# Page scores of the sample group: the queries held still on four column quarters, the turned keys of four pages moving, and the scores turned back

## Chip, core and metric

The kernel runs on one core of a Trainium2 chip. The metric is the time of one execution on the device in microseconds (us). Engines are named as in the profile: PE is TensorE (PEld its weight loads), DVE is VectorE, ACT is ScalarE, POOL is GpSimd, SP issues DMAs.

## The reference

One step of a decoder trunk of two layers. A prompt of 1024 new tokens and 8 sample sequences with one new token each (and 2048 past positions in 16 pages of 128) share all weights. Layer 0 mixes tokens by stick-breaking attention, layer 1 by forgetting attention; both have 16 heads of 64 with 4 key/value heads, and each layer ends in a convolutional feed-forward part.

```
h = rms_norm(x, norm_mix[i]);  q, k, v = split_qkv(h @ w_qkv[i])
k_all = concat(gather_pages(cache_k[i], page_table), k)       # sample group: 16 pages + 1 new row
z = einsum('bqngd,bsnd->bngqs', q, k_all) * Dh**-0.5          # the scores that the change is about
stick:  log_keep = log_sigmoid(-z);  w = exp(log_sigmoid(z) + sum of log_keep over later positions)
fox:    w = softmax(z + cum[pos] - cum[s])
x = x + einsum('bngqs,bsnd->bqngd', w, v_all) @ w_o[i]
x = x + conv_ffn(rms_norm(x, norm_ffn[i]))
```

The change touches z of the sample group alone: for each of 8 samples one query of 16 heads against 16 pages of 128 keys.

## The kernel before

Activations are kept transposed in SBUF, 1024 prompt columns and 8 sample columns. `attention(l)` is one phase per layer in which five engines run programs written out by hand; semaphores alone order them across engines, and each engine works strictly in its own order.

The prompt's attention goes in 128 steps: 16 heads of 8 query blocks of 128 rows. Within a head the blocks come in the order `ORDER = (0, 7, 1, 6, 2, 5, 3, 4)`, so a step at an odd place has a block index of 4 to 7, and one at an even place of 0 to 3. A step N of block i has (i+1) x 128 keys. On PE a turn of the loop for step N is: `turn(N)` (transposes of the weights in `rows`, one PSUM bank for every four key blocks, so one group for i below 4 and two from 4 on), then page transposes of the step, then `scores(N+3)`, then `values(N-1)`, then page scores. ACT and DVE empty the turned banks alternately into `wt` (`copy_turned`). In layer 0, ACT computes two sigmoids of the scores (`mid`), DVE a running product over them (`read_scores`, a scan), POOL a product. In layer 1, DVE adds the decay and takes the maximum (`read_scores`, a reduction), ACT the exponential, DVE the reciprocal, POOL the scaling. DVE reads the scores of step N+2 ahead of its copies of step N; one step before a new head's first scores are needed it also rounds that head's queries (`prepare`), and at each new key head the keys.

The samples' work is strewn over the same steps. A unit is two pages of a sample's keys; there are 64 units in a layer, at steps 2 to 59 (`k_step`). For a unit, SP loads two pages (`kpage`, six buffers), PE turns them (`turn_keys`, four 128x128 transposes into one bank), ACT copies the bank to `kt`, of which there are two, and one step later PE scores them (`score_keys`): the turned keys are stationary, 128 columns of them, and the 8 queries of a half of the heads in `qd` move. The result has keys on partitions and heads on columns, as all that follows needs it. After the 8 units of a sample DVE copies its scores from PSUM to `score` (`copy_scores`). Then come sums over later pages or the softmax, and from step 72 the value pages (`sum_values`).

All turned things share three PSUM banks, `t_ps`, in the order of the list `groups`. A group takes the bank of the third group before it, so `bank_free(g)` lets PE wait until ACT or DVE has copied that one:

```
def bank_free(g):
    if g >= TB:
        wait_copied(pe, g - TB)
```

Of the kernel before, what the change touches and what calls it, by code (L numbers as in the profile page):

```python
# [20 lines left out]
P = 128  # L21
# [8 lines left out]
def trunk_program(nc, x_prompt, x_sample, cache_k, cache_v, cache_logf, state_conv, page_table,  # L30
# [26 lines left out]
    with ctx:  # L57
# [1007 lines left out]
        UNITS = NB * NPAGE // 2  # L1065
        SEQ_UNITS = NPAGE // 2
        ROWS = 4
# [16 lines left out]
        def attention(l):  # L1084
# [20 lines left out]
            score = tile("score", [P, NB, NP1, NH])  # L1105
            qd = tile("qd", [P, HALVES, NB, HH])
            pages = tile("pages", [1, NB * NPAGE], I32)
# [7 lines left out]
            else:  # L1115
# [3 lines left out]
            kpage = [at(f"kpage{j}_{l}", [P, 2, KVD], XH + 4 * TILE + j * 2 * KVD * 4) for j in range(K_SLOTS)]  # L1119
            kt = [at(f"kt{j}_{l}", [P, 4 * P], XH + 4 * TILE + (K_SLOTS * KVD + j * 2 * P) * 8) for j in range(2)]  # L1120
            assert K_SLOTS * 2 * KVD * 4 + 2 * 4 * P * 4 <= 4 * TILE
            vpage = [at(f"vpage{j}_{l}", [P, 2, KVD], R1 + j * 2 * KVD * 4) for j in range(V_SLOTS)]
# [14 lines left out]
                [sem(f"dc_values{j}_{l}") for j in range(V_SLOTS)]  # L1137
            s_qd, s_ks, s_ev = sem(f"dc_queries_{l}"), sem(f"dc_scores_{l}"), sem(f"dc_scores_copied_{l}")
            s_ca, s_cd, s_cp = sem(f"dc_act_{l}"), sem(f"dc_dve_{l}"), sem(f"dc_pe_{l}")
# [9 lines left out]
            v_step = [V_FIRST + u * V_OVER // UNITS for u in range(UNITS)]  # L1149
            SCORED = k_step[-1] + 1  # L1150
            CUM = SCORED + 2 if fox else PER_TURN + 2
# [3 lines left out]
            def units_at(table, N):  # L1155
                return [u for u in range(UNITS) if table[u] == N]

            groups, of_step, of_unit = [], {}, {}
            for N in range(STEPS):
                for j0 in range(0, ORDER[N % ST] + 1, 4):  # L1160
                    of_step.setdefault(N, []).append(len(groups))
                    groups.append((j0, "act" if sum(1 for g in groups if g[0] is not None) % 2 == 0 else "dve"))
                for u in units_at(k_step, N):
                    of_unit[u] = len(groups)
                    groups.append((None, "act"))

            def copies(g):
# [30 lines left out]
            with phase() as block:  # L1198
# [27 lines left out]
                def _(pe):  # L1226
# [44 lines left out]
                    def turn_keys(u):  # L1271
                        g = of_unit[u]
                        bank_free(g)
                        pe.wait_ge(s_kp[u % K_SLOTS], 32 * (u // K_SLOTS + 1))
                        for j in range(2):
                            for hf in range(HALVES):
                                last = nc.tensor.transpose(t_ps[g % TB][:, (2 * j + hf) * P:(2 * j + hf + 1) * P],
                                                           kpage[u % K_SLOTS][:, j, hf * P:(hf + 1) * P], ident[:, :])
                        last.then_inc(s_t, 1)

                    def score_keys(u):
                        b, n = u // SEQ_UNITS, 2 * (u % SEQ_UNITS)
                        if u == 0:
                            pe.wait_ge(s_qd, 2)
                            if fox:
                                pe.wait_ge(s_tail, 2)
                        if n == 0 and b >= 1:
                            pe.wait_ge(s_ev, b)
                        wait_copied(pe, of_unit[u])
                        for j in range(2):  # L1290
                            for hf in range(HALVES):
                                c = b % 2 * NPAGE * NH + (n + j) * NH + hf * HH
                                last = nc.tensor.matmul(dec[:, c:c + HH], kt[u % 2][:, (2 * j + hf) * P:(2 * j + hf + 1) * P],
                                                        qd[:, hf, b, :], start=True, stop=True)
                        last.then_inc(s_ks, 1)

                    def score_new():
                        pe.wait_ge(s_qd, 2)
                        for b in range(NB):
                            for hf in range(HALVES):  # L1300
                                c = (b * HALVES + hf) * HH
                                last = nc.tensor.matmul(dec[0:1, c:c + HH], kvT[:, hf, SEQ + b:SEQ + b + 1], qd[:, hf, b, :],
                                                        start=True, stop=True)
                        last.then_inc(s_tail, 1)

                    def sum_keys(c):
                        if c == 0:
                            pe.wait_ge(s_ev, NB)
                            pe.wait_ge(s_cd, SUMS)
                        else:  # L1310
                            pe.wait_ge(s_cd, SUMS + c)
# [26 lines left out]
                    for N in range(STEPS + 1):  # L1338
# [6 lines left out]
                        if N >= 1:  # L1345
                            values(N - 1)
                            for u in units_at(k_step, N - 1):
                                score_keys(u)
                        for u in units_at(v_step, N):
# [18 lines left out]
                def _(dve):  # L1368
# [67 lines left out]

                    def copy_scores(b):
                        dve.wait_ge(s_ks, SEQ_UNITS * (b + 1))
                        src = dec[:, b % 2 * NPAGE * NH:(b % 2 + 1) * NPAGE * NH].rearrange("p (n h) -> p n h", h=NH)
                        nc.vector.tensor_copy(score[:, b, 0:NPAGE, :], src).then_inc(s_ev, 1)  # L1440

# [82 lines left out]
                    for side in range(2):  # L1524
                        for par in range(2):
                            last = nc.vector.tensor_copy(
                                qd[half(side)].rearrange("p f b (s j r) -> p f s j r b", s=2, j=2)[:, :, side, :, par, :],
                                sample_columns(qT, side, par))
# [11 lines left out]
                    for N in range(STEPS + 1):  # L1540
                        if fox and N + 1 < STEPS:
                            invert(N + 1)
                        if N + 2 < STEPS:
                            read_scores(N + 2)
                        if N < STEPS:
                            copy_turned(N)
                        if heads_prepared_at(N) is not None:
                            prepare(heads_prepared_at(N))
                        if N >= 1 and (N - 1) % ST >= ST - 2:
                            store_o(N - 1)  # L1550
                        for u in units_at(k_step, N - 1):
                            if u % SEQ_UNITS == SEQ_UNITS - 1:
                                copy_scores(u // SEQ_UNITS)
                        if fox and N == PER_TURN - ST:
# [11 lines left out]
                def _(act):  # L1566
# [46 lines left out]
                    def copy_keys(u):  # L1613
                        g = of_unit[u]
                        if u >= 2:
                            act.wait_ge(s_ks, u - 1)
                        act.wait_ge(s_t, g + 1)
                        nc.scalar.activation(kt[u % 2][:, :], t_ps[g % TB][:, :], ACT.Copy).then_inc(s_ta, 1)

                    def soft_plus():  # L1620
                        act.wait_ge(s_ev, NB)
                        act.wait_ge(s_q, 2 * HG)
# [26 lines left out]
                    ahead = 2 if fox else 3  # L1649
                    for N in range(STEPS):  # L1650
                        copy_turned(N)
                        for u in units_at(k_step, N):
# [77 lines left out]
```

## Time and profile before

| | |
|---|---|
| three runs | 3201.16, 3202.53, 3210.64 us, median 3202.53 |
| the profiled execution | 3201.7 us, its span 3199.7 us |
| busy in the span | PE 3002.5 us (94%), DVE 1401.9 (44%), ACT 901.0 (28%), POOL 888.6 (28%) |

The page gives busy time by engine, the granted clock of PE in tenths of full speed, and the costliest groups of instructions. PE is busy nearly everywhere, so what the change makes PE do counts at once, and what it lets PE wait for counts too; the other engines have room, and only the moment at which they get to a thing matters.

### The profile page before, as it was taken

Reading aid. Unit: us, or ns where it says so; the run is one execution under the profiler, and the core shown is the slowest. Engines: PE = TensorE matmul, PEld = TensorE weight load, DVE = VectorE, ACT = ScalarE, POOL = GpSimd, SP = SyncE. Lnnn points to the kernel's source line nnn. Section 1 sums busy time; section 2 is a strip of 40 time slices with the busy share of each in tenths; the row PEclk is TensorE's granted clock in tenths of the full one; section 3 lists DMA queues with packets and bytes.
Section 4 is the critical chain, followed back from the end, with each engine's and each line's share of the span. In section 5 each row is a group of like instructions: output and inputs, shape, how many; then the busy total and the mean of one; then the engine's idle time right before and its main releaser. Section 6 shows DMA issues by size and latency. Waiting matters only on the chain. (4 is left out here: it accounts for less than half of the span.)

```text
span 3199.7 us, 50554 instructions
## 1 busy us (share of the span) xinstructions
PE 3002.5 (94%) x19894; PEld 2870.9 (90%) x19894; DVE 1401.9 (44%) x1823; ACT 901.0 (28%) x1229; POOL 888.6 (28%) x415
## 2 busy tenths in 40 slices
PE   6989997998999999999999899899899999999994
PEld 5978886888999999999989789788899999999994
DVE  5144445554434334334361444655443433343435
ACT  3035554443211111111230354433321121111111
POOL 2112222332122322222311244445312222222220
PEclk8989897999999999999999899999999999999997
DMA  2112211221111111111101233133111111111111
GB/s 99 55 54 65 65 41 47 83 84 53 40 40 53 47 51 47 39 39 53 54 31 48 82 102 94 56 110 106 57 40 40 40 53 53 53 39 39 40 39 53
DMA packets 177557, 182.75 MB, mean 57 GB/s; under 512 B 31927, under 2 KB 167569, under 8 KB 177334
## 3 DMA queue, kind: packets, MB, share of 16 engines
q1 hardware_dynamic: 175086, 172.14, 17.5%
q10 hardware_dynamic: 2304, 8.39, 0.8%
q8 instruction: 104, 1.70, 0.2%
q14 instruction: 63, 0.52, 0.1%
HBM read 171.67 MB, written 8.99 MB: 56 GB/s over the span
## 5 line engine op out<-in xcount | busy, mean ns | idle before, releaser
L334 PE MATMUL psum<-x_hi,w_hi 128*128 128x344 f32 x2688 | 578.1, 324 | 4.2 <-issue 2.7
L334 PE MATMUL psum<-x_lo,w_hi 128*128 128x344 f32 x2688 | 571.9, 321 | 0.0
L334 PE MATMUL psum<-x_hi,w_lo 128*128 128x344 f32 x2688 | 569.0, 320 | 0.0
L334 PEld LDWEIGHTS psum<-x_hi,w_hi 128*128 128x128 f32 x2688 | 451.7, 189 | 7.5 <-issue 4.7
L334 PEld LDWEIGHTS psum<-x_lo,w_hi 128*128 128x128 f32 x2688 | 456.2, 190 | 0.0
L334 PEld LDWEIGHTS psum<-x_hi,w_lo 128*128 128x128 f32 x2688 | 449.6, 188 | 0.0
L867 DVE TENSOR_TENSOR xT<-psum,xT 128x1032 f32<-128x1032 f32 x176 | 217.0, 1233 | 287.2 <-PE psum L334 287.2
L713 POOL TENSOR_TENSOR w_lo<-raw,w_hi 128x2048 fp32r<-128x2048 f32 x44 | 203.3, 4621 | 419.9 <-ACT w_hi L709 419.9
L1267 PE MATMUL psum<-wt,tokv 128*64 128x128 f32 x2304 | 319.2, 286 | 0.0
L1671 POOL TENSOR_SCALAR rows<-rows,stat 128x128 f32<-128x128 f32 (+7 forms) x128 | 220.5, 1726 | 309.8 <-DVE stat L1420 309.7
L854 POOL TENSOR_TENSOR act_lo<-gate,act_hi 128x1032 fp32r<-128x1032 f32 x44 | 106.3, 2415 | 717.5 <-ACT act_hi L825 717.5
L1267 PEld LDWEIGHTS psum<-wt,tokv 128*64 128x64 f32 x2304 | 255.9, 141 | 31.9 <-issue 12.0
L1678 POOL TENSOR_TENSOR rows<-rows,keep 128x128 f32<-128x128 f32 (+7 forms) x128 | 154.3, 1214 | 434.5 <-DVE keep L1403 434.5
L334 PE MATMUL psum<-act_hi,down_hi 128*128 128x344 f32 x1056 | 225.6, 322 | 12.8 <-issue 12.8
L334 PE MATMUL psum<-act_hi,down_lo 128*128 128x344 f32 x1056 | 225.4, 322 | 0.0
L334 PE MATMUL psum<-act_lo,down_hi 128*128 128x344 f32 x1056 | 223.8, 320 | 0.0
L1403 DVE TENSOR_TENSOR_SCAN keep<-psum,zero 128x128 f32<-128x128 f32 (+7 forms) x128 | 173.3, 1355 | 114.2 <-ACT psum L1601 112.9
L875 DVE TENSOR_TENSOR a_pad<-psum,rstd 128x1032 f32<-128x1032 f32 x44 | 54.2, 1233 | 384.2 <-PE psum L334 384.2
L709 ACT ACTIVATE w_hi<-raw 128x2048 fp32r<-128x2048 f32 x44 | 84.4, 1918 | 416.0 <-DMA raw<-in_ffn_w_b_dram 209.5
L1239 PE MATMUL psum<-k_hi,queries 128*128 128x512 f32 (+3 forms) x384 | 160.4, 418 | 41.0 <-DVE keep L1403 25.6
L1254 PE MATMUL psum<-ident,rows 128*128 128x128 f32 x1152 | 183.6, 288 | 11.5 <-POOL rows L1671 9.6
L823 ACT ACTIVATE conv<-conv 128x1032 f32<-128x1032 f32 x44 | 47.0, 1068 | 519.5 <-DVE conv L898 519.5
(202 smaller groups left out, 4410.8 us busy)
## 6 DMA issues: line engine op xcount, KB each, us to landing
kpage<-in_cache_k_dram SPq DMA_DIRECT2D x256, 128.0 KB, 2.0
vpage<-in_cache_v_dram SPq DMA_DIRECT2D x256, 128.0 KB, 2.0
raw<-in_ffn_w_a_dram SPq DMA_DIRECT2D x22, 1024.0 KB
raw<-in_ffn_w_b_dram SPq DMA_DIRECT2D x22, 1024.0 KB
raw<-in_ffn_w_down_dram SPq DMA_DIRECT2D x22, 1024.0 KB
raw<-in_w_qkv_dram SPq DMA_DIRECT2D x10, 1024.0 KB, 4.8
ncum<-ncum_scratch ACTq DMA_DIRECT2D x16, 512.0 KB, 4.0
raw<-in_w_o_dram SPq DMA_DIRECT2D x6, 1024.0 KB, 4.9
```

Source lines behind the costliest of these rows:

```text
L334: last = nc.tensor.matmul(out[:, c, 0:NG], w[:, k, cols], r(k)[:, c * NG:(c + 1) * NG], start=(k == 0 and part == 0), stop=(k == kt - 1 an ...
L709: nc.scalar.activation(dst, src, ACT.Copy).then_inc(self.s_hi, 1)
L713: nc.gpsimd.tensor_tensor(dst, src, hi.bitcast(F32), ALU.subtract).then_inc(self.s_lo, 1)
L854: nc.gpsimd.tensor_tensor(act_lo[:, m, :], gate[m][:, :], act_hi[:, m, :].bitcast(F32), ALU.subtract).then_inc(s_alo, 1)
L867: nc.vector.tensor_tensor(thirds(xT[:, t, :]), acc[side][:, :, 0:NG], thirds(xT[:, t, :]), ALU.add).then_inc(s_added, 1)
L875: nc.vector.tensor_tensor(thirds(a_pad[m][:, 2:2 + TOK]), acc[0][:, :, 0:NG], thirds(rstd[:, :]), ALU.mult).then_inc(s_acopy, 1)
L1239: nc.tensor.matmul(out[:, c0:c1], q, keys[:, h // HG % 2, c0:c1], start=(keys is k_hi), stop=(keys is k_lo))
L1254: last = nc.tensor.transpose(t_ps[g % TB][:, (j - j0) * P:(j - j0 + 1) * P], rows[N % ROWS][:, j * P:(j + 1) * P], ident[:, :])
L1267: last = nc.tensor.matmul(o_ps[side][:, i % 4 * P:(i % 4 + 1) * P], tokv[:, j, kv], wt[N % 2][:, j * P:(j + 1) * P], start=(j == 0), stop= ...
L1403: nc.vector.tensor_tensor_scan(backwards(keep[N % PB], SEQ - L, SEQ), backwards(buffer_of(N), 0, L), zero[:, 0:L], 1.0, ALU.mult, ALU.add) ...
L1671: nc.gpsimd.tensor_scalar(rows[N % ROWS][:, 0:L], rows[N % ROWS][:, 0:L], stat[:, N % 4, 3:4], None, ALU.mult).then_inc(s_w, 1)
L1678: nc.gpsimd.tensor_tensor(rows[N % ROWS][:, 0:L], rows[N % ROWS][:, 0:L], keep[N % PB][:, SEQ - L + 1:SEQ + 1], ALU.mult).then_inc(s_w, 1)
```

## The change

For two units (a quad, four pages) the queries become the stationary side: `qd` is padded from 8 to 32 columns, and each of four matmuls has 32 stationary columns, 256 moving columns (two pages' turned keys of one half of the heads) and its own 32 partitions of PSUM. The scores then stand with heads on partitions. ACT copies them to `score_rows`, PE turns them back by two transposes into a bank of the ring, and DVE copies them from there into `score`, in two pieces. A quad is scored in the step after its second unit's pages were turned (`k_scored`), and turned a step later (`k_turned`). `kt` has four buffers instead of two. The scores are complete two steps later than before (`SCORED`); ACT's soft-plus in layer 0 and the sums and softmax in layer 1 (`CUM`) move with them.

```diff
-            qd = tile("qd", [P, HALVES, NB, HH])
+            qd = tile("qd", [P, HALVES, NB, 32])
+            score_rows = tile("score_rows", [P, 2 * P])
...
+            kt += [tile(f"kt{j}", [P, 4 * P], end=W) for j in range(2, 4)]
...
-            SCORED = k_step[-1] + 1
+            k_scored = [k_step[u] + 1 for u in range(1, UNITS, 2)]
+            k_turned = [step + 1 for step in k_scored]
+            QUADS = UNITS // 2
+            SCORED = k_turned[-1] + 1
...
+                for quad in units_at(k_turned, N):
+                    of_quad[quad] = len(groups)
+                    groups.append((None, "dve"))
...
-                    def score_keys(u):
...
-                        for j in range(2):
-                            for hf in range(HALVES):
-                                c = b % 2 * NPAGE * NH + (n + j) * NH + hf * HH
-                                last = nc.tensor.matmul(dec[:, c:c + HH], kt[u % 2][:, (2 * j + hf) * P:(2 * j + hf + 1) * P],
-                                                        qd[:, hf, b, :], start=True, stop=True)
+                    def score_keys(quad):
...
+                        else:
+                            pe.wait_ge(s_rows, quad)
+                        wait_copied(pe, of_unit[2 * quad + 1])
+                        for u in (2 * quad, 2 * quad + 1):
+                            for hf in range(HALVES):
+                                q = u % 2 * HALVES + hf
+                                last = nc.tensor.matmul(dec[q * 32:(q + 1) * 32, 0:2 * P], qd[:, hf, b, :],
+                                                        kt[u % 4][:, hf * 2 * P:(hf + 1) * 2 * P], start=True, stop=True)
+                        last.then_inc(s_ks, 1)
+
+                    def turn_scores(quad):
+                        g = of_quad[quad]
+                        bank_free(g)
+                        pe.wait_ge(s_rows, quad + 1)
+                        for j in range(2):
+                            last = nc.tensor.transpose(t_ps[g % TB][:, j * P:(j + 1) * P], score_rows[:, j * P:(j + 1) * P], ident[:, :])
+                        last.then_inc(s_t, 1)
...
-                            for u in units_at(k_step, N - 1):
-                                score_keys(u)
+                            for quad in units_at(k_scored, N):
+                                score_keys(quad)
+                            for quad in units_at(k_turned, N):
+                                turn_scores(quad)
...
+                        dve.wait_ge(s_t, g + 1)
+                        src = t_ps[g % TB][:, 0:2 * P].rearrange("p (j u f r) -> p u j f r", j=2, u=2, f=HALVES)[:, :, :, :, 0:HH]
+                        out = score[:, b, n0:n0 + 4, :].rearrange("p (u j) (f r) -> p u j f r", u=2, f=HALVES)
+                        for u in range(2):
+                            last = nc.vector.tensor_copy(out[:, u], src[:, u])
+                        last.then_inc(s_td, 1)
...
+                        for quad in units_at(k_turned, N - 1):
+                            copy_scores(quad)
                         if N < STEPS:
                             copy_turned(N)
...
+                    def copy_score_rows(quad):
+                        act.wait_ge(s_ks, quad + 1)
+                        if quad >= 1:
+                            act.wait_ge(s_t, of_quad[quad - 1] + 1)
+                        nc.scalar.activation(score_rows[:, :], dec[:, 0:2 * P], ACT.Copy).then_inc(s_rows, 1)
...
+                        for quad in units_at(k_scored, N - 1):
+                            copy_score_rows(quad)
                         copy_turned(N)
```

PE in layer 0, from the values of step 4 (`wt0`) to the turn of step 7 (`rows3`), before. `rows`, `kpage`, `kt` and `wt` carry their buffer's number.

```order
L1267 MATMUL psum<-wt0_0_1518,tokv_73 64x128 x3
L1293 MATMUL psum<-qd_0_1510,kt1_0_1527 128x8 x4
L1254 MATMUL psum<-ident_49,rows2_0_1507 128x128 x4
L1277 MATMUL psum<-ident_49,kpage5_0_1525 128x128 x4
L1239 MATMUL psum<-k_hi_0_1499,queries1_0_1502 128x512
L1239 MATMUL psum<-k_lo_0_1500,queries1_0_1502 128x512
L1239 MATMUL psum<-k_hi_0_1499,queries1_0_1502 128x512
L1239 MATMUL psum<-k_lo_0_1500,queries1_0_1502 128x512
L1241 MATMUL psum<-mask_q_0_1504,ident_q_0_1503 128x128
L1267 MATMUL psum<-wt1_0_1519,tokv_73 64x128 x6
L1293 MATMUL psum<-qd_0_1510,kt0_0_1526 128x8 x4
L1254 MATMUL psum<-ident_49,rows3_0_1508 128x128 x5
```

The same place on PE in the changed kernel, from the quad scored in step 5 to the turn of step 7.

```order
L1302 MATMUL psum<-kt2_0_1529,qd_0_1510 32x256 x2
L1302 MATMUL psum<-kt3_0_1530,qd_0_1510 32x256 x2
L1262 MATMUL psum<-ident_49,rows2_0_1507 128x128 x4
L1285 MATMUL psum<-ident_49,kpage5_0_1526 128x128 x4
L1247 MATMUL psum<-k_hi_0_1499,queries1_0_1502 128x512
L1247 MATMUL psum<-k_lo_0_1500,queries1_0_1502 128x512
L1247 MATMUL psum<-k_hi_0_1499,queries1_0_1502 128x512
L1247 MATMUL psum<-k_lo_0_1500,queries1_0_1502 128x512
L1249 MATMUL psum<-mask_q_0_1504,ident_q_0_1503 128x128
L1275 MATMUL psum<-wt1_0_1520,tokv_73 64x128 x6
L1311 MATMUL psum<-ident_49,score_rows_0_1511 128x128 x2
L1262 MATMUL psum<-ident_49,rows3_0_1508 128x128 x5
```

The score matmuls of single units at the end of each step are replaced by four wide ones in one step and two transposes in the next. The transposes of `score_rows` take a bank between the page transposes of step 6 and the two groups of step 7.

DVE in layer 0, from the copy of step 6's turned weights to the scan of step 10's scores, before.

```order
L1429 COPY wt0_0_1518<-psum 128x512
L1385 TENSOR_TENSOR queries0_0_1501<-qT_67,queries0_0_1501 64x1024
L1403 SCALAR_TENSOR_TENSOR keep0_0_1514<-psum,zero_0_1517 128x1024
L1429 COPY wt1_0_1519<-psum 128x128
L1434 TENSOR_SCALAR oT_69<-psum 64x512
L1403 SCALAR_TENSOR_TENSOR keep1_0_1515<-psum,zero_0_1517 128x256
```

The same place on DVE in the changed kernel.

```order
L1448 COPY wt0_0_1519<-psum 128x512
L1404 TENSOR_TENSOR queries0_0_1501<-qT_67,queries0_0_1501 64x1024
L1422 SCALAR_TENSOR_TENSOR keep0_0_1515<-psum,zero_0_1518 128x1024
L1463 COPY score_0_1509<-psum 128x32 x2
L1448 COPY wt1_0_1520<-psum 128x128
L1453 TENSOR_SCALAR oT_69<-psum 64x512
```

The copies of a quad that PE turned in step 6 stand behind the scan of step 9's scores (1024 keys), which itself stands behind the rounding of the next head's queries, and ahead of the copy of step 7's weights.

## Rows read from the trace of the kernel before

**Rows 1.** The page's head.

```profile
span 3199.7 us, 50554 instructions
```

**Rows 2.** Windows: the stretches with page scores in layers 0 and 1.

```profile
core 0: us, PE busy (x) PEld busy (x) DVE busy (x) ACT busy (x) POOL busy (x), PEclk, DMA share, GB/s
214.80:471.50 256.70, 244.97 (x1806) 220.43 (x1806) 123.29 (x133) 134.23 (x235) 71.89 (x60) 0.93 0.21 61
1802.00:2031.40 229.40, 227.35 (x1796) 205.97 (x1795) 105.00 (x308) 110.38 (x233) 100.51 (x59) 0.99 0.34 90
```

**Rows 3.** Waits of PE, 214.8 to 471.5 us: total, times, longest.

```profile
PE psum L1277 <- DVE wt L1429: 9.2, 8, 2.9
PE psum L1277 <- ACT wt L1610: 2.5, 1, 2.5
```

**Rows 4.** Timeline of PE, layer 0: start, length, instruction.

```profile
404.68 1.74 PE L1267 MATMUL psum<-wt,tokv 128*64 128x128 f32 x14
406.35 1.06 PE L1293 MATMUL psum<-qd,kt 128*128 128x8 f32 x8
407.26 0.85 PE L1254 MATMUL psum<-ident,rows 128*128 128x128 f32 x6
407.95 0.60 PE L1277 MATMUL psum<-ident,kpage 128*128 128x128 f32 x4
```

**Rows 5.** Timeline of PE, layer 1, sums over keys.

```profile
2054.89 1.02 PE L1315 MATMUL psum<-later,ones 128*128 128x512 f32 x2
2055.75 0.38 PE L1254 MATMUL psum<-ident,rows 128*128 128x128 f32 x2
```

**Rows 6.** Groups by line and form: busy us, mean ns, idle before.

```profile
L1293 PE MATMUL psum<-qd,kt 128*128 128x8 f32 x1024 | 136.3, 261 | 0.0
...
L1380 DVE TENSOR_TENSOR k_lo<-kvT,k_hi 64x1024 fp32r<-64x1024 f32 x16 | 19.6, 1226 | 3.2 <-ACT k_hi L1571 2.7
...
L1610 ACT ACTIVATE wt<-psum 128x256 f32<-128x256 f32 x32 | 12.3, 385 | 72.5 <-PE psum L1254 72.5
...
L1429 DVE COPY wt<-psum 128x128 f32<-128x128 f32 x32 | 9.0, 280 | 7.3 <-PE psum L1254 7.3
```

**Rows 7.** Timeline, layer 0: PE in step 7 (L1254, L1277), DVE ahead of it.

```profile
234.27 1.07 ACT L1576 ACTIVATE queries<-qT 64x1024 fp32r<-64x1024 f32 x1
...
234.51 0.74 PE L1254 MATMUL psum<-ident,rows 128*128 128x128 f32 x5
...
235.09 0.60 PE L1277 MATMUL psum<-ident,kpage 128*128 128x128 f32 x4
...
235.37 1.22 DVE L1385 TENSOR_TENSOR queries<-qT,queries 64x1024 fp32r<-64x1024 f32 x1 [3.79 <-ACT queries L1576]
...
236.63 2.29 DVE L1403 TENSOR_TENSOR_SCAN keep<-psum,zero 128x1024 f32<-128x1024 f32 x1
```

**Rows 8.** Timeline, layer 0: step 9's page transposes and step 11's scan.

```profile
244.23 2.02 DVE L1403 TENSOR_TENSOR_SCAN keep<-psum,zero 128x896 f32<-128x896 f32 x1
...
245.22 0.60 PE L1277 MATMUL psum<-ident,kpage 128*128 128x128 f32 x4
```

**Rows 9.** Timeline, layer 0: step 5's page transposes and step 7's scan.

```profile
225.85 1.49 DVE L1403 TENSOR_TENSOR_SCAN keep<-psum,zero 128x640 f32<-128x640 f32 x1 [1.01 <-ACT psum L1601]
...
227.63 0.60 PE L1277 MATMUL psum<-ident,kpage 128*128 128x128 f32 x4
```

**Rows 10.** Timeline, layer 1: step 7's page transposes and step 9's reduction.

```profile
1819.70 1.21 DVE L1412 CUSTOM_DVE_ANT_0 rows<-psum,ncum 128x1024 f32<-128x1024 f32 x1
...
1820.18 0.60 PE L1277 MATMUL psum<-ident,kpage 128*128 128x128 f32 x4
...
1820.95 0.15 DVE L1415 TENSOR_SCALAR stat<-stat 128x1 f32<-128x1 f32 x1
```

**Rows 11.** Windows: layer 0 after the wait of 2.5 us, columns as in rows 2.

```profile
342.40:359.50 17.10, 17.10 (x75) 15.35 (x73) 8.04 (x9) 5.25 (x11) 3.88 (x3) 0.50 0.13 39
```

**Rows 12.** Timeline of PE, layer 0, step 64: a wait for a scan.

```profile
490.74 0.79 PE L1239 MATMUL psum<-k_hi,queries 128*128 128x512 f32 x1 [12.02 <-DVE keep L1403]
```

More of the change, by code:

```diff
@@ L1065, in trunk_program @@
         UNITS = NB * NPAGE // 2
-        SEQ_UNITS = NPAGE // 2
+        SEQ_UNITS, SEQ_QUADS = NPAGE // 2, NPAGE // 4
         ROWS = 4
@@ L1137, in attention @@
                 [sem(f"dc_values{j}_{l}") for j in range(V_SLOTS)]
[L1138 removed]
+            s_qd, s_ks, s_rows = sem(f"dc_queries_{l}"), sem(f"dc_scores_{l}"), sem(f"dc_scores_copied_{l}")
             s_ca, s_cd, s_cp = sem(f"dc_act_{l}"), sem(f"dc_dve_{l}"), sem(f"dc_pe_{l}")
@@ L1155, in units_at @@
             def units_at(table, N):
-                return [u for u in range(UNITS) if table[u] == N]
-            groups, of_step, of_unit = [], {}, {}
+                return [u for u, step in enumerate(table) if step == N]
+            groups, of_step, of_unit, of_quad = [], {}, {}, {}
             for N in range(STEPS):
@@ L1276, in turn_keys @@
                             for hf in range(HALVES):
-                                last = nc.tensor.transpose(t_ps[g % TB][:, (2 * j + hf) * P:(2 * j + hf + 1) * P],
+                                last = nc.tensor.transpose(t_ps[g % TB][:, (2 * hf + j) * P:(2 * hf + j + 1) * P],
                                                            kpage[u % K_SLOTS][:, j, hf * P:(hf + 1) * P], ident[:, :])
                         last.then_inc(s_t, 1)
-                    def score_keys(u):
-                        b, n = u // SEQ_UNITS, 2 * (u % SEQ_UNITS)
-                        if u == 0:
+                    def score_keys(quad):
+                        b = quad // SEQ_QUADS
+                        if quad == 0:
                             pe.wait_ge(s_qd, 2)
@@ L1301, in score_new @@
                                 c = (b * HALVES + hf) * HH
-                                last = nc.tensor.matmul(dec[0:1, c:c + HH], kvT[:, hf, SEQ + b:SEQ + b + 1], qd[:, hf, b, :],
+                                last = nc.tensor.matmul(dec[0:1, c:c + HH], kvT[:, hf, SEQ + b:SEQ + b + 1], qd[:, hf, b, 0:HH],
                                                         start=True, stop=True)
@@ L1307, in sum_keys @@
                         if c == 0:
-                            pe.wait_ge(s_ev, NB)
+                            wait_copied(pe, of_quad[QUADS - 1])
                             pe.wait_ge(s_cd, SUMS)
@@ L1435, in store_o, with copy_scores @@
                             .then_inc(s_o, 1)
[L1437 to L1440, printed above, removed]
+                    def copy_scores(quad):
+                        g = of_quad[quad]
+                        b, n0 = quad // SEQ_QUADS, 4 * (quad % SEQ_QUADS)
+                        dve.wait_ge(s_t, g + 1)
[4 more added lines that the diff above has]
+                        last.then_inc(s_td, 1)
                     def sums_of_later_pages():
@@ L1526, in _ @@
                             last = nc.vector.tensor_copy(
-                                qd[half(side)].rearrange("p f b (s j r) -> p f s j r b", s=2, j=2)[:, :, side, :, par, :],
+                                qd[half(side), :, :, 0:HH].rearrange("p f b (s j r) -> p f s j r b", s=2, j=2)[:, :, side, :, par, :],
                                 sample_columns(qT, side, par))
@@ L1550, in _ @@
                             store_o(N - 1)
-                        for u in units_at(k_step, N - 1):
-                            if u % SEQ_UNITS == SEQ_UNITS - 1:
-                                copy_scores(u // SEQ_UNITS)
                         if fox and N == PER_TURN - ST:
@@ L1614, in copy_keys @@
                         g = of_unit[u]
-                        if u >= 2:
-                            act.wait_ge(s_ks, u - 1)
+                        if u >= 4:
+                            act.wait_ge(s_ks, (u - 4) // 2 + 1)
                         act.wait_ge(s_t, g + 1)
-                        nc.scalar.activation(kt[u % 2][:, :], t_ps[g % TB][:, :], ACT.Copy).then_inc(s_ta, 1)
+                        nc.scalar.activation(kt[u % 4][:, :], t_ps[g % TB][:, :], ACT.Copy).then_inc(s_ta, 1)
+                    def copy_score_rows(quad):
[3 more added lines that the diff above has]
+                        nc.scalar.activation(score_rows[:, :], dec[:, 0:2 * P], ACT.Copy).then_inc(s_rows, 1)
                     def soft_plus():
-                        act.wait_ge(s_ev, NB)
+                        wait_copied(act, of_quad[QUADS - 1])
                         act.wait_ge(s_q, 2 * HG)
```

4 lines of the change are left out of this document (removed).

## The prediction

> **What bounds the kernel now.** I read the page's head first: the span is 3199.7 us [rows 1]. The profiled execution's own time is 3201.7 us, 2.0 us more, and 0.8 us below the median of the runs shown, 3202.53 us; the sum is made against 3201.7. Then I cut out, by the first transposed page and the last score matmul of each layer, the two stretches in which pages are scored: 256.7 us in layer 0 and 229.4 us in layer 1 [rows 2]. TensorE is busy in 245.0 and 227.4 us of them, VectorE and ScalarE in about half. So TensorE sets the pace in layer 1. In layer 0 something else takes part: the granted clock is 0.93 there, and the view of the waits shows TensorE held back by copies out of the three rotating PSUM banks, 9.2 us in 8 waits on VectorE's copy of turned weights and 2.5 us in one on ScalarE's [rows 3]. Both layers score 64 units in 58 steps, so 27.3 us of span and 17.6 of TensorE's idle time are what these banks and the lower clock make of layer 0.
>
> **What the change takes from TensorE and what it gives.** A unit (two pages) has four score matmuls, in the trace eight records, because every float32 matmul that is no transpose shows two. From the first of them to the next operation it is 407.26 - 406.35 = 0.91 us, 0.114 us a record, with 8 moving columns [rows 4]. There are 1024 records in 128 units [rows 6]: 128 x 0.91 = 116.5 us go.
>
> For a quad (two units) come four matmuls of 256 moving columns, eight records, and two transposes. Six transposes take 407.95 - 407.26 = 0.69 us, 0.115 each [rows 4]: 128 x 0.115 = 14.7 us. A record with 256 columns is not in the trace. Two with 512 take 2055.75 - 2054.89 = 0.86 us, 0.43 each [rows 5], and fourteen with 128 take 406.35 - 404.68 = 1.67 us, 0.12 each at most [rows 4]; halfway by columns that is 0.215. What a quad takes then depends on whether quarters of the array work at the same time, and no row shows that, since no two matmuls on different column parts follow each other in this trace. The bounds: all eight records one behind the other, 8 x 0.215 = 1.72 us; all four quarters side by side, the two records of each still in order, 2 x 0.215 = 0.43 us. I take five lengths, 1.08 us: the two records of a quarter cannot overlap, they are neighbours in the queue, and if TensorE starts in order, only the second of one quarter can run beside the first of the next. Over 64 quads: 110, 69 or 27.5 us.
>
> Going from the 64-column matmuls of values to the full array leaves 1.67 - 14 x 0.114 = 0.07 us over in [rows 4]. That turn-over was there before the score matmuls and stays; a second one, from quarters back to the full array, is new. I take 0.09 us, 64 x 0.09 = 6 us, with bounds of 0 and twice that. TensorE's own work thus changes by 69 + 14.7 + 6 - 116.5 = -27 us (+14 if serial, -68 if side by side).
>
> **What the other engines get.** ScalarE copies 128x256 scores per quad; the same form takes 0.385 us [rows 6], 25 us in all, into idle halves of the stretches [rows 2]. VectorE loses 16 copies of a sample's scores and gets 128 copies of 128x32, each between 0.15 us, the one-element operation [rows 10], and 0.28 us, the 128x128 copy [rows 6]; near the low end, 0.18, so 0.36 us a quad. As work both are covered. As places in a queue they are not.
>
> **The wait that the change adds.** A quad's turned scores take a place in the ring of three banks, behind the page transposes of the same step N. VectorE empties it in its turn N+1, behind the scan (layer 1: the reduction) of the scores of step N+3, as the listing of VectorE shows. TensorE needs that bank again three groups later. Where N is even, step N+1 has a block index of 4 or more, so two groups, and the third is the page transposes of step N+1, which come right behind. So TensorE, with the scores of step N+4, values and the next turn queued behind it, waits for a scan that it did not wait for before. By the schedule 16 of the 32 quads in each layer are turned at even steps (4 to 12, 24 to 32, 42 to 52). Where N is odd, the third group is a step further on, and there is time.
>
> The price of one: when VectorE would be done, less when TensorE comes. TensorE comes 0.91 - 0.23 = 0.68 us earlier than in the trace, because the scores of the unit before are gone from that step and two transposes stand there.
> - N = 6 of a head, layer 0: VectorE prepares the next head's queries behind ScalarE's 1.07 us, then scans 1024 keys until 236.63 + 2.29 = 238.92; with 0.36 for the copies 239.28. TensorE reaches its page transposes at 235.09 - 0.68 = 234.41 [rows 7]. Wait 4.9 us, at steps 6 and 46; at step 30 two key halves are rounded as well, 2 x 1.23 [rows 6], so 7.3. Together 17.1.
> - N = 0: 244.23 + 2.02 + 0.36 = 246.61 against 245.22 - 0.68 = 244.54 [rows 8]: 2.1 us, at four steps 8.3.
> - N = 4: 225.85 + 1.49 + 0.36 = 227.70 against 227.63 - 0.68 = 226.95 [rows 9]: 0.75 us; N = 2 taken alike, nine steps, 6.8.
>
> That is 32 us in layer 0. Where the ring made TensorE wait for the weights one group later, the new wait takes that one's place: 2.5 and three of 1.15 (9.2 / 8) us [rows 3], 6 us. Net +26.
>
> In layer 1 the reduction is shorter than the scan. N = 6: 1820.95 + 0.15 + 0.36 = 1821.46 against 1820.18 - 0.68 = 1819.50 [rows 10], 2.0 us twice and 4.4 with keys; N = 0 at half of that, 1.0 four times; N = 2 and 4 none. That is 12; ScalarE's score copy lies ahead of the exponential that VectorE waits for there, which I put at 2. Net +14. All of it has bounds: nothing, if the copies come early enough, and half as much again.
>
> **The clock.** A layer-0 wait of 2.5 us [rows 3] is followed by 17.1 us at a clock of 0.50, 1.2 instead of 2.4 GHz, at which matmuls take twice as long [rows 11]. A mean of 0.93 over 256.7 us means 36 us at half, 18 us lost, 2 us for each of the 9 waits. Nineteen more waits of 0.7 us and over (12 and 7 net) would lose 38; but where TensorE is slow, the next bank is free when it comes, so I take half, +18, with 0 and 38 as ends.
>
> **The later steps.** Scores are complete two steps later. In layer 0 ScalarE's soft-plus then no longer stands just ahead of the next head's keys, where TensorE now waits 12.0 us [rows 12]; that may give back half, 6. In layer 1 the chain of the softmax starts two steps later against a fixed start of the value pages, which may cost a step, 229.4 / 58 = 4.0 us. I take 0 for both. The four key buffers instead of two free ScalarE from a wait; it costs TensorE nothing now and gains nothing.
>
> **Sum:** 3201.7 - 27 + 26 + 14 + 18 = 3233 us. For the likeliest case alone I would give 3210 to 3255.
>
> **Rivals.**
> 1. *The quarters run one after another.* For it: nothing in the trace overlaps two matmuls. The waits stay, TensorE's work grows by 14 instead of shrinking by 27: 3274 us.
> 2. *All four run side by side.* 3233 - 41 = 3192 us, still eaten up for the most part by waits. With 58 us of waits and clock against it, the change breaks even at (116.5 - 20.7 - 58) / 64 = 0.59 us for a quad's four matmuls. The Trainium skill, TensorEngine Tiling (Array Packing), section Performance Considerations, recommends just this swap of the streaming and the stationary side with 4x column tiling for few streamed columns; by it this rival is the outcome. No run here shows it yet. 
> 3. *The banks do not bind* (the other side, faster). Once TensorE has waited at one place, scans and copies are early at the next; if VectorE's copy is in front of TensorE at nearly all even steps, the waits go and the clock stays: 3201.7 - 27 = 3175 us. It decides the sign as soon as waits and clock together cost less than 27 us. Against it: scan N+3 cannot start before its scores, which TensorE makes in step N, so an earlier wait doesn't help it, and at N = 0 and 6 the order alone makes 2 us and more.
>
> **How the numbers follow.** Chances: forecast 0.42, rival 1 0.28, rival 2 0.15, rival 3 0.15. The range leaves out rival 3 and the far ends: 3183 to 3285 us. A measurement here tells 0.3%, 9.6 us, from no change. Faster has rival 3 and half of rival 2, 0.22; same the other half and the low edge of the forecast, 0.13; slower the rest, 0.65.
>
> **What the new profile would show.** Right: page transposes waiting on VectorE's score copy, some 30 us in layer 0 and some 14 in layer 1, the longest at steps 7, 31 and 47; a stretch of layer 0 with a clock below 0.93; a quad's four matmuls within about 1.1 us. Wrong: four matmuls in 0.5 us or in 1.7 us; layer 1's stretch shorter than 229 us with its clock still 0.99; waits on the score copy of a few us only.

## The result, and the profile after

The changed kernel is faster by 0.7%: 3182.53 us median of 12 runs (3161.88 to 3196.25) against 3203.73 us of 12 runs of the kernel before (3195.81 to 3210.64), a ratio of 0.9933 with an interval of 0.9909 to 0.9958. The forecast was 3233 us, slower.

The profiled execution took 3196.25 us, the longest of the twelve, so its span must not be read against [rows 1] as if it were the median. The page's head and the first row of busy time:

```profile
span 3194.2 us, 50132 instructions
...
PE 2966.2 (93%) x19510; PEld 2802.0 (88%) x19510; DVE 1413.0 (44%) x1935; ACT 925.7 (29%) x1293; POOL 889.9 (28%) x415
```

TensorE is busy 36 us less (2966.2 against 3002.5) and the span is 5.5 us shorter. Where the rest went is seen in the windows after, columns as in [rows 2]: page scores of layer 0, what follows them to the end of the prompt's steps, and the same two in layer 1.

```profile
213.80:460.70 246.90, 211.01 (x1611) 169.97 (x1611) 127.92 (x189) 146.54 (x266) 72.14 (x60) 0.93 0.22 63
460.70:740.00 279.30, 255.48 (x1655) 222.48 (x1650) 144.79 (x162) 119.51 (x194) 77.13 (x65) 0.85 0.21 61
1804.00:2018.80 214.80, 201.24 (x1616) 163.91 (x1615) 111.58 (x370) 124.35 (x267) 103.40 (x60) 0.98 0.37 96
2018.80:2256.00 237.20, 227.58 (x1641) 198.41 (x1639) 132.30 (x358) 86.00 (x187) 110.15 (x65) 0.95 0.30 88
```

The second and fourth of these stretches in the kernel before:

```profile
471.50:737.00 265.50, 237.72 (x1648) 206.54 (x1647) 144.44 (x160) 119.12 (x193) 76.82 (x65) 0.90 0.23 64
...
2031.40:2260.00 228.60, 219.05 (x1640) 190.34 (x1638) 132.99 (x361) 86.08 (x186) 111.42 (x65) 0.99 0.31 91
```

The scoring stretches are 9.8 and 14.6 us shorter than those of [rows 2]. The stretches behind them, in which the change adds next to no work, are 13.8 and 8.6 us longer, with almost the same instructions (1655 and 1641 against 1648 and 1640), more busy time for them and a lower granted clock: 0.85 for 0.90 and 0.95 for 0.99.

I compared these two stretches, from the last score matmul to the last product with `wt`, in all nine traces of this document. In layer 0 the clock differs from execution to execution: 0.85 to 0.94 in the seven with the change, 0.90 and 0.91 in the two without (the kernel before and `e5_kt4`). In layer 1 it goes with the change: the seven take 243.7 to 245.7 us at 0.95 to 0.97, the two without 236.9 us at 0.99. One thing that differs there is the wait for ScalarE's exponential of the samples' scores, ahead of the first value pages. It is 2.9 us now, and 13.7 us at half clock (1.2 GHz) come with it:

```profile
2069.64 3.58 PE L1345 MATMUL psum<-score,vpage 128*128 128x8 f32 x16 [2.91 <-ACT score L1664]
...
2068.80:2082.50 13.70, 12.87 (x56) 12.00 (x57) 6.86 (x12) 3.76 (x9) 5.30 (x3) 0.50 0.25 67
```

The same place in the kernel before:

```profile
2079.27 1.95 PE L1328 MATMUL psum<-score,vpage 128*128 128x8 f32 x16 [0.99 <-ACT score L1635]
...
2079.30:2093.00 13.70, 13.70 (x105) 12.25 (x106) 10.23 (x20) 5.02 (x12) 5.82 (x4) 1.00 0.29 86
```

In all seven, 10.2 to 13.7 us at half clock come with this wait of 2.9 to 3.0 us; in the two without the change it is 1.0 us and the clock stays full. Over the twelve runs the time goes with the mean granted clock of the run: 3161.9 us at 0.966, 3171.3 at 0.962, 3180.5 at 0.958, 3192 to 3196 at 0.954 and 0.955.

What a quad costs is in the timeline of PE, layer 0 (L1302 scores a quad, L1311 turns it, L1285 are the page transposes, L1262 and L1275 `turn` and values):

```profile
219.38 0.65 PE L1275 MATMUL psum<-wt,tokv 128*64 128x128 f32 x4
219.96 0.64 PE L1302 MATMUL psum<-kt,qd 128*32 128x256 f32 x8
220.53 0.55 PE L1262 MATMUL psum<-ident,rows 128*128 128x128 f32 x3
...
231.13 0.44 PE L1311 MATMUL psum<-ident,score_rows 128*128 128x128 f32 x2
231.40 0.71 PE L1262 MATMUL psum<-ident,rows 128*128 128x128 f32 x5
236.67 1.12 PE L1285 MATMUL psum<-ident,kpage 128*128 128x128 f32 x4 [4.56 <-DVE score L1463]
...
240.15 1.08 PE L1302 MATMUL psum<-kt,qd 128*32 128x256 f32 x8
241.16 0.48 PE L1262 MATMUL psum<-ident,rows 128*128 128x128 f32 x1
```

From the first record of a quad to the next operation it is 220.53 - 219.96 = 0.57 us, at half clock 241.16 - 240.15 = 1.01. In the trace's single records the eight start 7, 6, 7, 220, 7, 6 and 7 ns apart, and the next operation 310 ns after the last: four start within 20 ns, then a second four 0.22 us after the last of these. The last distance is 0.09 us longer than the one between the two fours. So 0.48 us are the matmuls and 0.09 the turn-over. The transposes take 231.40 - 231.13 = 0.27 us a quad. The row at 236.67 is the predicted wait at step 7.

The waits of PE, 214 to 475 us and 1800 to 2022 us:

```profile
PE psum L1285 <- DVE score L1463: 26.5, 14, 7.1
PE psum L1262 <- DVE wt L1448: 8.0, 4, 2.2
PE psum L1247 <- DVE keep L1422: 5.5, 1, 5.5
...
PE psum L1285 <- DVE score L1463: 12.2, 8, 4.3
PE psum L1262 <- POOL rows L1702: 1.9, 2, 1.6
```

They answer to [rows 3]: page transposes now wait for VectorE's copy of turned scores, 26.5 us in layer 0 and 12.2 us in layer 1.

### The profile page after: what moved, and what is told of

It is laid out like the page before. It is cut to its first block and busy times, and to the rows that moved or that the text cites. A ratio compares the mean times of both kernels' runs of the same rounds, so it can differ in the third digit from the quotient of the medians.

```text
span 3194.2 us, 50132 instructions
## 1 busy us (share of the span) xinstructions
PE 2966.2 (93%) x19510; PEld 2802.0 (88%) x19510; DVE 1413.0 (44%) x1935; ACT 925.7 (29%) x1293; POOL 889.9 (28%) x415
## 5 line engine op out<-in xcount | busy, mean ns | idle before, releaser
L1275 PE MATMUL psum<-wt,tokv 128*64 128x128 f32 x2304 | 328.1, 291 | 0.0
L1275 PEld LDWEIGHTS psum<-wt,tokv 128*64 128x64 f32 x2304 | 263.8, 145 | 32.4 <-issue 11.1
L1262 PE MATMUL psum<-ident,rows 128*128 128x128 f32 x1152 | 185.9, 291 | 18.4 <-POOL rows L1702 9.6
L1247 PE MATMUL psum<-k_hi,queries 128*128 128x512 f32 (+3 forms) x384 | 162.2, 422 | 37.0 <-DVE keep L1422 21.6
```

The lines of the kernel that those rows point to most:

```text
L1247: nc.tensor.matmul(out[:, c0:c1], q, keys[:, h // HG % 2, c0:c1], start=(keys is k_hi), stop=(keys is k_lo))
L1262: last = nc.tensor.transpose(t_ps[g % TB][:, (j - j0) * P:(j - j0 + 1) * P], rows[N % ROWS][:, j * P:(j + 1) * P], ident[:, :])
L1275: last = nc.tensor.matmul(o_ps[side][:, i % 4 * P:(i % 4 + 1) * P], tokv[:, j, kv], wt[N % 2][:, j * P:(j + 1) * P], start=(j == 0), stop= ...
```

## Experiments

What these rows suggest: a quad's four matmuls run side by side in two passes, so TensorE's work shrinks by far more than forecast, and the waits on the ring come about as forecast and eat half of it. Against it: the waits are harmless, or the order of the instructions or the small stationary side, and not the four quarters, makes the matmuls short. Each expectation names the theories that its run tells apart.

**VectorE's turn reordered** (`e1_front`). The copies of a quad's scores go ahead of the scan or reduction of the step.

```diff
+                        for quad in units_at(k_turned, N - 1):
+                            copy_scores(quad)
                         if N + 2 < STEPS:
                             read_scores(N + 2)
-                        for quad in units_at(k_turned, N - 1):
-                            copy_scores(quad)
```

> The changed kernel, but VectorE copies a quad's turned scores at the head of its turn, ahead of the scan (layer 1: the reduction) of the scores three steps on, not behind it. Theory A (the ring of three banks holds TensorE up for that scan): the 39 us in which page transposes wait for the score copy (26.5 in layer 0, 12.2 in layer 1) fall to under 10; scans begin up to 0.4 us later, which shows as small waits elsewhere; the time is 15 to 35 us below the 3182.5 of the changed kernel, 3148 to 3168. Rival (those waits only stand in for others that come right behind, the scan's own chain being the limit): the waits go over to turned weights, scans and rows in about the same sum, and the time stays within 8 us of 3182.

Measured: 3151.21 us against 3197.24, ratio 0.9856 (0.9834 to 0.9879). The waits of PE from 214 to 475 us, with that on the score copy down from 26.5 to 9.5 us:

```profile
PE psum L1262 <- DVE wt L1448: 9.9, 7, 2.2
PE psum L1285 <- DVE score L1463: 9.5, 3, 4.9
PE psum L1247 <- DVE keep L1422: 8.4, 2, 5.5
```

Nothing but the place in VectorE's queue is different, so these waits do cost the changed kernel time, and most of them come from standing behind the scan. In layer 1, 3.8 us are left of 12.2. The 13.3 us in all are more than the 10 expected at most, and the time is inside the range.

**Turned scores outside the ring** (`e2_own`). The two transposes write to columns 256 to 511 of `dec`, with semaphores of their own, and a quad takes no place in the ring any more.

```diff
-                        bank_free(g)
...
-                            last = nc.tensor.transpose(t_ps[g % TB][:, j * P:(j + 1) * P], score_rows[:, j * P:(j + 1) * P], ident[:, :])
-                        last.then_inc(s_t, 1)
+                            last = nc.tensor.transpose(dec[:, (2 + j) * P:(3 + j) * P], score_rows[:, j * P:(j + 1) * P], ident[:, :])
+                        last.then_inc(s_tq, 1)
```

> The changed kernel, but the turned scores go to the free half of the score bank instead of a place in the ring; the next quad's score matmuls then wait for VectorE's copy, some 3 us further on in TensorE's order. Theory A: page transposes no longer wait for VectorE's score copy at all, at most 8 us of waits appear at the score matmuls; 20 to 38 us below the changed kernel, 3145 to 3163, as good as the copy ahead of the scan or better. Rival (as before): within 8 us of 3182.

Measured: 3147.35 us, ratio 0.9841 (0.9822 to 0.9859). The waits from 214 to 475 us, and one from 1780 to 2022 us:

```profile
PE psum L1303 <- DVE score L1463: 8.4, 5, 2.9
PE psum L1283 <- DVE wt L1449: 7.4, 5, 2.0
...
PE psum L1283 <- DMA kpage<-in_cache_k_dram: 12.2, 10, 2.7
```

The page transposes no longer wait for scores; what is left of that wait is the next quad's score matmuls (L1303) waiting until the turned scores before are stored. In layer 1 TensorE now gets to the pages before they have landed.

**Each quarter's matmul in two neighbouring halves** (`e3_halves`): 128 columns each, the second right behind the first on the same quarter. This aims at the step of the prediction that says neighbours of a quarter hold back all that follow.

```diff
-                                last = nc.tensor.matmul(dec[q * 32:(q + 1) * 32, 0:2 * P], qd[:, hf, b, :],
-                                                        kt[u % 4][:, hf * 2 * P:(hf + 1) * 2 * P], start=True, stop=True)
+                                for j in range(2):
+                                    last = nc.tensor.matmul(dec[q * 32:(q + 1) * 32, j * P:(j + 1) * P], qd[:, hf, b, :],
+                                                            kt[u % 4][:, (2 * hf + j) * P:(2 * hf + j + 1) * P], start=True, stop=True)
```

> The changed kernel, but each quarter's matmul of 256 columns is two of 128 that follow each other, the same columns and products in all. Theory A (a matmul starts beside its predecessor only if that one works on another quarter, and starts are in order): the eight neighbours on one quarter run one after the other, at 0.11 us a record 13 lengths, 1.4 us and 0.09 for the turn-over in place of the 0.57 us that a quad takes in the changed kernel: TensorE has 60 us more, the time is 3225 to 3250. Rival (each quarter works off its own queue, whatever the order): four lengths of 0.11 and the turn-over, 0.55 us, the time within 8 us of 3182.

Measured: 3176.87 us, ratio 0.9934 (0.9914 to 0.9954), the same as the change. Timeline of PE, layer 0:

```profile
220.95 0.66 PE L1303 MATMUL psum<-kt,qd 128*32 128x128 f32 x16
221.54 0.55 PE L1262 MATMUL psum<-ident,rows 128*128 128x128 f32 x3
```

Sixteen records, in fours that start within 42 ns, last 0.59 us with the turn-over, against 0.57. Of the two expectations the one in which order costs something fell: neighbours on a quarter don't hold the others back.

**Units scored alone** (`e4_pairs`): the two matmuls of a unit in its own step, so two quarters at a time instead of four.

```diff
...
-                            for quad in units_at(k_scored, N):
-                                score_keys(quad)
+                            for u in units_at(k_step, N - 1):
+                                score_unit(u)
```

> The changed kernel, but a unit's two matmuls are done in the step after its own pages were turned, as before the change, so that two quarters at a time have work. Reading 1 (the two bursts of four records in a quad are the two passes, all four quarters side by side): two quarters take two lengths of 0.215 and the turn-over, 0.53 us a unit, 1.06 a quad in place of 0.57: with a second turn-over TensorE has 30 us more, 3205 to 3220. Reading 2 (the bursts are the two units, and both passes of a quarter start together): one length and the turn-over, 0.31 us a unit, 0.62 a quad, the time within 10 us of 3186.

Measured: 3189.96 us, ratio 0.9979 (0.9964 to 0.9993), a gain of 0.2% where the change has 0.7%. Timeline of PE, layer 0:

```profile
225.88 0.63 PE L1301 MATMUL psum<-kt,qd 128*32 128x256 f32 x4
226.44 0.66 PE L1262 MATMUL psum<-ident,rows 128*128 128x128 f32 x4
```

Two matmuls last 0.56 us, as long as four. The second pair of quarters is free, and a unit alone costs what a quad costs: 128 x 0.557 = 71.3 us in all, against 64 x 0.570 = 36.5. These are the lengths of reading 1, but the time is not: 3190 us instead of 3205 to 3220, a value that reading 2 allows. The waits are why. That on the score copy is 19.8 us in layer 0, where the change has 26.5, and 8.8 in layer 1, where it has 12.2, so that of 35 us more matmul time 17 show at a like clock (table below).

```profile
PE psum L1285 <- DVE score L1463: 19.8, 8, 6.5
```

**All four on one quarter** (`e7_one_quarter`), the control. The results of three of the four are lost by it.

```diff
-                                q = u % 2 * HALVES + hf
+                                q = u % 2 * HALVES + hf if quad == 0 else 0
```

> The changed kernel with all four matmuls of a quad (from the second quad on) writing to the same 32 partitions instead of to four quarters; the scores of three of the four are therefore overwritten, and the samples' outputs are not the reference's. Instructions, waits and data moved are the same. Theory A (it is the four quarters side by side that make a quad's eight records last 0.48 us): the records come one behind the other, about 0.22 us apart, 8 x 0.22 + 0.09 = 1.85 us for a quad instead of 0.57, 64 x 1.28 = 82 us more work of TensorE; by the kernel with units scored alone, in which about half of the added matmul time showed, 40 to 80 us more than the changed kernel: ratio to the kernel before 1.005 to 1.020. Rival (32 stationary columns alone make it short, wherever they are): a quad's records within 0.6 us and a ratio of 0.990 to 0.996.

Measured: 3238.43 us against 3202.68, ratio 1.0117 (1.0095 to 1.0140), slower. Timeline of PE, layer 0:

```profile
229.03 1.91 PE L1302 MATMUL psum<-kt,qd 128*32 128x256 f32 x8
230.88 0.66 PE L1262 MATMUL psum<-ident,rows 128*128 128x128 f32 x4
```

Eight records 0.216 us apart (the first two 0.24), 1.85 us a quad. The same instructions in the same order on four quarters or on one: 0.57 or 1.85 us, faster or slower than before. Without the four side by side nothing of the gain is left. All four matmuls also write the same PSUM addresses here, which could be what keeps them apart; against that, the sixteen records of `e3_halves`, half of which go to other addresses of the same quarters, come in four fours and not in two eights.

**Four key buffers alone** (`e5_kt4`), on the kernel before.

```diff
+            kt += [tile(f"kt{j}", [P, 4 * P], end=W) for j in range(2, 4)]
...
-                        if u >= 2:
-                            act.wait_ge(s_ks, u - 1)
+                        if u >= 4:
+                            act.wait_ge(s_ks, u - 3)
...
```

> The kernel before with one part of the change alone: four buffers of turned keys instead of two, so that ScalarE copies a unit's turned pages without waiting until the unit two before it is scored. The prediction put this at nothing. Theory A (matmuls shorter, waits on the ring added, nothing else of size): 3197 to 3210 us where the kernel before is at 3203, a ratio of 0.998 to 1.002, and the waits in layer 0 on VectorE's copy of turned weights stay near 9 us. Rival (the buffers free ScalarE early enough to empty the ring sooner, and part of the change's gain is theirs): 3175 to 3192 us, and the wait on ScalarE's copies and some of those on VectorE's go.

Measured: 3184.74 us against 3196.83, ratio 0.9961 (0.9936 to 0.9986): inside the rival's range, near its slow end, with an interval that reaches theory A's 0.998. Waits of PE, 214 to 475 us:

```profile
PE psum L1278 <- DVE wt L1430: 5.3, 6, 1.2
PE psum L1278 <- ACT wt L1611: 2.5, 1, 2.5
```

Of the 9.2 us of [rows 3] 5.3 are left, as the rival has it; the wait on ScalarE's copy, which it says goes, is still 2.5 us. That explains some 4 us of the 12; the mean clock of its runs is 0.9658 against 0.9634, which goes with the rest.

**Both cures together** (`e6_own_front`): the edits of `e1_front` and `e2_own`.

> The changed kernel with both cures together: turned scores in PSUM columns of their own, and VectorE's copy of them ahead of its reading of the scores of step N+3. Each alone gave 3147 to 3151 us against 3197 of the kernel before. Theory A (the two take away the same waits): 3143 to 3151 us, ratio 0.983 to 0.986, within 5 us of each alone; the wait of a quad's score matmuls on the stored copy (8.4 us in 5 waits in layer 0 with the columns alone) goes below 3 us, and the waits on page loads in layer 1 (12.2 us) stay. Rival (the waits are additive, and each cure leaves some that the other takes): 3125 to 3142 us, ratio 0.977 to 0.982.

Measured: 3147.92 us, ratio 0.9828 (0.9802 to 0.9853). The wait of the score matmuls in layer 0, and that on pages in layer 1:

```profile
PE psum L1303 <- DVE score L1463: 1.3, 2, 0.7
...
PE psum L1283 <- DMA kpage<-in_cache_k_dram: 12.7, 14, 2.1
```

It is as fast as each cure alone. The wait it takes away comes back in layer 0 as waits on copies of turned weights (L1283, 11.2 us for the 7.4 of `e2_own`); those on pages not yet landed in layer 1 stay (12.7 us for 12.2).

**All of them in one sum.** Within each kernel, over all 83 runs whose clock is known, the time rises by 25.8 us when the run's mean granted clock falls by 0.01 (15 to 32 us in single kernels). I bring every kernel's mean to a clock of 0.963 with that; the kernel before then stands at 3200.2, 3201.6 and 3202.0 us on three chips, 3201.0 in the mean. Beside it I set what the traces say without any run time: the change in scoring and turning (quad 0.570 + 0.274 us, times 64, against 128 x 0.914 us before, and so on), and the change in TensorE's waits for other engines and for pages in both attention phases (61.3 us before, without those at a phase's start; one execution of each kernel).

| kernel | scoring, us | waits, us | sum | measured at 0.963 | mean clock |
|---|---|---|---|---|---|
| changed | -63 | +32 | -31 | -31 | 0.9584 |
| e3_halves | -61 | +33 | -28 | -30 | 0.9607 |
| e4_pairs | -28 | +17 | -11 | -14 | 0.9606 |
| e1_front | -63 | +9 | -54 | -48 | 0.9637 |
| e2_own | -63 | +11 | -52 | -48 | 0.9652 |
| e6_own_front | -63 | +12 | -51 | -50 | 0.9642 |
| e7_one_quarter | +19 | +24 | +43 | +40 | 0.9635 |
| e5_kt4 | 0 | -5 | -5 | -6 | 0.9658 |

Two terms hold all eight within some 6 us, at a like clock. What the change does to the clock itself is left out of this sum.

## Why the prediction was wrong

**The step that failed** is "I take five lengths, 1.08 us". It was two lengths, 0.48 us: the lower of the two bounds. Of the two reasons given, one holds (the two records of a quarter follow each other, 0.22 us apart, 0.215 was the estimate of a length, and in `e4_pairs` two quarters still take two lengths) and the other, that only the second record of a quarter can run beside the first of the next, does not. `e3_halves` shows that neighbours on a quarter are no hindrance, `e7_one_quarter` that a single quarter gives the upper bound (1.85 - 0.09 = 1.76 us, estimated 1.72). The five lengths were an argument about the order of starts; no row had shown it, and rival 2, the lower bound, had the right mechanism and a sum of 3192 us, with a break-even at 0.59 us, but a chance of only 0.15.

The Trainium skill, TensorEngine Tiling (Array Packing), section Performance Considerations, recommends this swap with 4x column tiling; the trace agrees, with 0.48 us for four against 1.76 on one quarter. The remark of the Trainium skill in the same section that copies out of PSUM may then become the limit agrees in so far as TensorE now waits 26.5 and 12.2 us for such copies, though by `e1_front` more for their place behind a scan than for their length. The rule of the Trainium skill, TensorE: Matmul & The Clock Gate, Part 3, that matmuls start and end in program order, could not be tested on starts, as the records do not tell which quarter each belongs to; the five lengths that I drew from it fell. If a quarter takes one record at a time, as in `e7_one_quarter`, the four records of `e3_halves` that start together are on four quarters, which is not the order in which the kernel writes them; in which order they stood in TensorE's queue no run tells.

**The waits** behind the score copy were right in place and size. In layer 0, 32 us were forecast and 26.5 came; at step 7, 4.9 us were forecast and 4.56 came. In layer 1, 12 were forecast and 12.2 came. The 8.0 us on `turn` are another thing, which the prediction does not have: it says that at odd N there is time. For the quad's own bank there is, in layer 0, but the quad's place in the ring moves the others: the one group of weights turned in the next step needs the bank that the page transposes behind it needed before. At steps 16, 24, 40 and 56 the page transposes waited 6.0 us for VectorE's copies of turned weights; now `turn` waits 8.0 us for the same copies. Step 16, before and after:

```profile
273.22 0.66 PE L1277 MATMUL psum<-ident,kpage 128*128 128x128 f32 x4 [0.99 <-DVE wt L1429]
...
273.53 0.45 PE L1262 MATMUL psum<-ident,rows 128*128 128x128 f32 x1 [2.18 <-DVE wt L1448]
```

In all, TensorE waits 36.6 us for the ring in layer 0 where it waited 12.7, 24 us more for the 26 forecast. For both layers, net, I had 26 + 14 = 40 us; the phases have 32. The row that fell out of the net is [rows 12]: the wait for the scan is now 5.5 us where it was 12.0, more than the half that I had mentioned and put at 0, although over the phase waits on `keep` fell only from 25.6 to 21.6 us. In layer 1 the later softmax, also put at 0, did cost something: ScalarE's part of the wait is 2.9 instead of 1.0 us, and with the half clock behind it the stretch is 7 to 9 us longer in every trace with the change, where the prediction had mentioned 4.0. The two terms put at 0 were not nothing; they nearly cancel.

**The clock** was put at +18 us. The changed kernel's runs have a mean clock of 0.9584; the kernel before, in the runs beside the experiments, has 0.9626 to 0.9634. The difference times 25.8 us per 0.01 is 11 to 13 us. On one and the same chip `e3_halves`, with the waits of the change, has 0.9607 against 0.9634, 7 us. So the term was of the right sign and too large, and the place was wrong: layer 0's scoring stretch still has 0.93, and what falls in every trace with the change is layer 1 behind the scores, from 0.99 to between 0.95 and 0.97. Kernels with fewer waits have the higher clocks in the table, but with much added work (`e7_one_quarter`) the clock is high as well; that the waits lower it was not shown.

**Four buffers** were said to gain nothing; alone they gave 6 us at a like clock.

**A misreading.** The 17.6 us that the prediction calls TensorE's idle time are the difference of its busy times in [rows 2], 245.0 and 227.4 us. Its idle times there, 11.7 and 2.0 us, differ by 9.7. The sum does not use the figure.

**The sum.** At a like clock the forecast was -27 + 40 = +13 us and -31 came. Of the 44 between, 64 x (1.08 - 0.48) = 38 are the failed step, less 3 for the transposes that turn back (0.274 a quad instead of 0.23), and 8 the waits. The sign hung on the one duration that the trace before did not hold.

## What to carry over

When a sum turns on one duration that no row shows, and its bounds lie on both sides of break-even, an argument for a value in between is no measurement: keep both ends as cases of like weight. Four small products on different column quarters cost no more here than two, 0.57 us for 0.56, so fill all four before issuing. A result that leaves through a shared ring of banks stands behind everything ahead of its copy on the engine that empties it: place the copy first, or give it a bank of its own; here that was worth 17 us more at a like clock, the ratio going from 0.993 to between 0.983 and 0.986.

## What was not expected of the hardware

- A float32 matmul of 32 stationary and 256 moving columns shows two records 0.22 us apart; four on four quarters start within 20 ns of each other in each of the two passes. One pair takes 0.56 us, four 0.57, four on one quarter 1.85, each with 0.09 us of turn-over to the full array behind it.
- The changed kernel's runs spread over 34 us (3161.9 to 3196.3), with mean granted clocks from 0.966 to 0.954. Within a kernel 0.01 of clock is worth 25.8 us, and reading all kernels at one clock brings the kernel before on three chips to within 2 us.
